# A two-block decoder kernel on one core: how the per-layer embedding projections leave PSUM, and where the sixth tile of the gating products stands

## The reference, cut to what matters

```
g = gelu(y + d_skip * u)
val, gate = split(g @ w_glu, 2)
return val * sigmoid(gate)
```

```
x = x + conv_ffn(h, ffn_w_up[i], ffn_conv_w[i], ffn_conv_b[i], ffn_w_down[i])
gate = sigmoid(rms_norm_2(x, ple_norm[i]) @ ple_w_gate[i])
x = x + gate * (p[i] @ ple_w_proj[i])
```

## Time and profile before

| | |
|---|---|
| median of 3 runs | 2107.18 us (2101.96 to 2107.51) |
| the profiled execution | 2104.71 us, of which span 2102.9 us |
| granted TensorE clock, mean | 0.974 of full speed |
| PE busy | 1988.4 us (95%), 9640 matmuls |
| DVE busy | 1220.0 us (58%) |
| ACT busy | 852.2 us (41%) |
| POOL busy | 442.8 us (21%) |
| chain that ended last | PE 84%, DVE 8%, ACT 5% |

### The profile page before, as it was taken

The page is one execution under the profiler, slowest core; times in us unless marked ns, Lnnn a source line. Parts: engine busy times, 40 slices in busy tenths (PEclk is TensorE's granted clock), DMA queues, the critical chain, the costliest instruction groups (busy, mean ns, idle before and its releaser), DMA issues.

```text
span 2102.9 us, 26554 instructions
## 1 busy us (share of the span) xinstructions
PE 1988.4 (95%) x9640; PEld 1615.3 (77%) x9640; DVE 1220.0 (58%) x1727; ACT 852.2 (41%) x1343; POOL 442.8 (21%) x609
## 2 busy tenths in 40 slices
PE   8999999999999888999999989798777999999988
PEld 8998678888887777877877868686666777878877
DVE  5445465555455994477466456734556666465555
ACT  4323342222235884344244235534665444243333
POOL 3110039998815451100000001100000200000010
PEclk9999899999999999999999999899899999999999
DMA  4221023264442332222323223221111123223232
GB/s 153 84 79 65 21 90 107 85 213 157 167 167 88 121 128 83 87 82 94 105 84 107 81 91 110 92 91 45 51 51 36 61 90 104 87 90 110 80 104 97
DMA packets 65077, 201.64 MB, mean 96 GB/s; under 512 B 6422, under 2 KB 19222, under 8 KB 63948
## 3 DMA queue, kind: packets, MB, share of 16 engines
q1 hardware_dynamic: 57372, 166.39, 23.6%
q0 software_dynamic: 7600, 33.84, 4.5%
HBM read 184.44 MB, written 15.77 MB: 95 GB/s over the span
## 4 chain that ended last, share of the span: by engine, by line
PE 84%; DVE 8%; ACT 5%; issue 2%; DMA 1%; POOL 1%; SPq 0%; ACTq 0%; DVEq 0%; POOLq 0%
PE ps L449 60%; PE ps L587 7%; PE ps L1729 5%; PE ps L738 2%; PE ps L1843 1%; PE ps L438 1%; PE ps L813 1%; DVE w_lo L428 1%; ACT w_hi L424 1%; ACT t L2033 1%; PE ps L1957 1%; DMA cp<-mix_cp 1%; POOL t L529 1%; DMA raw<-in_wstream 1%; PE ps L769 0%
## 5 line engine op out<-in xcount | busy, mean ns | idle before, releaser
L428 DVE TENSOR_TENSOR w_lo<-raw,w_hi 128x1024 fp32r<-128x1024 f32 x308 | 396.7, 1291 | 169.0 <-ACT w_hi L424 168.5
L449 PE MATMUL ps<-x_hi,w_hi 128*128 128x512 f32 x1152 | 458.8, 398 | 3.9 <-DVE w_lo L428 2.6
L449 PE MATMUL ps<-x_lo,w_hi 128*128 128x512 f32 x1152 | 455.7, 396 | 0.0
L449 PE MATMUL ps<-x_hi,w_lo 128*128 128x512 f32 x1152 | 453.5, 394 | 0.0
L424 ACT ACTIVATE w_hi<-raw 128x1024 fp32r<-128x1024 f32 x308 | 322.1, 1049 | 247.5 <-DMA raw<-in_wstream 154.2
L449 PE MATMUL ps<-a_hi,w_hi 128*128 128x512 f32 x704 | 279.8, 397 | 7.7 <-DVE pp L1584 4.8
L449 PE MATMUL ps<-a_hi,w_lo 128*128 128x512 f32 x704 | 279.8, 397 | 0.0
L449 PE MATMUL ps<-a_lo,w_hi 128*128 128x512 f32 x704 | 279.6, 397 | 0.0
L529 POOL TENSOR_TENSOR t<-t,sq 128x512 f32<-128x512 f32 x49 | 72.6, 1483 | 938.4 <-ACT sq L520 936.4
L449 PEld LDWEIGHTS ps<-x_hi,w_hi 128*128 128x128 f32 x1152 | 216.4, 188 | 69.0 <-issue 11.4
L449 PEld LDWEIGHTS ps<-x_hi,w_lo 128*128 128x128 f32 x1152 | 216.7, 188 | 49.8
(11 more groups left out here) (402 smaller groups left out, 3043.0 us busy)
## 6 DMA issues: line engine op xcount, KB each, us to landing
raw<-in_wstream SPq DMA_DIRECT2D x308, 512.0 KB, 3.3
ev<-mix_ev POOLq DMA_DIRECT2D x8, 1024.0 KB, 5.0
mix_cp<-c_p POOLq DMA_DIRECT2D x8, 640.0 KB, 3.4
cp<-mix_cp POOLq DMA_DIRECT2D x8, 640.0 KB, 6.3
mix_ev<-v_b POOLq DMA_DIRECT2D x8, 512.0 KB, 3.5
fall<-fall POOLq DMA_DIRECT2D x4, 544.0 KB, 4.9
h<-in_xT SPq DMA_DIRECT2D x4, 528.0 KB, 6.2
mix_ev<-e_r POOLq DMA_DIRECT2D x1, 2048.0 KB, 9.4
```

The costliest lines, as they stand in the source:

```text
L428: e.tensor_tensor(w_lo[:, u.slot, :], raw[:, u.c % 2, :], w_hi[:, u.slot, :], ALU.subtract)\
L449: last = e.matmul(ps[:, bank, :], wt[:, u.slot, w], x[:, k0 + k, 0:SEQ], start=(k == 0 and n == 0), stop=(k == kt - 1 and n == 2))
```

## The change

The side projection now uses all eight banks. Unit u0 writes banks 4 to 7, unit u0+1 writes banks 0 to 3 in the order in which the next units will need them: `side_bank` gives (u0 + 2 + q) % 4, that is 2, 3, 0, 1 in layer 0 and 0, 1, 2, 3 in layer 1. Each bank's group of 6 matmuls signals when it is done (`pp_mm` for the first three of a unit, `unit_mm` for the fourth), and DVE copies each bank by itself (four copies of 512 columns instead of one of 2048; `pp_ev` counts the first three of a unit, `unit_ev` the fourth). The first side unit no longer waits for `unit_ev`, the second waits for `unit_ev >= u0`, and behind the two PE waits until six of the eight copies are done instead of all. In the gating stage `glu_open_pe` takes a range of tiles: banks 0 and 1 are opened with tiles 0 to 4 ahead of the last tile's output products, and tile 5 follows behind them.

```diff
-    def glu_open_pe(e, s):
+    def glu_open_pe(e, s, k0, k1):
         u = Unit(U_GLU + s)
-        e.wait_ge(lo_ok, u.n(1))
-        e.wait_ge(unit_ev, U_GLU)
-        if s >= 2:
-            e.wait_ge(v_ev, KT)
-        for k in range(GLU_K):
+        if k0 == 0:
+            e.wait_ge(lo_ok, u.n(1))
+            e.wait_ge(unit_ev, U_GLU)
+            if s >= 2:
+                e.wait_ge(v_ev, KT)
+        for k in range(k0, k1):
             if s == 0:
                 e.wait_ge(g_lo, k + 1)
             product(e, u, s, a_hi, a_lo, k, KT)
...
                 u = Unit(u0 + s)
-                e.wait_ge(unit_mm, u.n(1))
-                e.tensor_copy(pp[:, 4 * s:4 * s + 4, :], ps[:, 0:4, :]).then_inc(unit_ev, 1)
+                for q in range(4):
+                    if q < 3:
+                        e.wait_ge(pp_mm, 6 * layer + 3 * s + q + 1)
+                    else:
+                        e.wait_ge(unit_mm, u.n(1))
+                    e.tensor_copy(pp[:, 4 * s + q, :], ps[:, side_bank(u0, s, q), :])                        .then_inc(pp_ev if q < 3 else unit_ev, 1)
                 split_ahead(e, u, split_lo)
         else:
             e.wait_ge(plo_ok, layer + 1)
             for s in range(2):
                 u = Unit(u0 + s)
                 e.wait_ge(lo_ok, u.n(1))
-                e.wait_ge(unit_ev, u.n())
+                if s:
+                    e.wait_ge(unit_ev, u0)
                 for q in range(4):
-                    last = products(e, u, q, p_hi, p_lo, kt=2, w0=2 * q)
-                last.then_inc(unit_mm, 1)
-            e.wait_ge(unit_ev, u0 + 2)
+                    products(e, u, side_bank(u0, s, q), p_hi, p_lo, kt=2, w0=2 * q)                        .then_inc(pp_mm if q < 3 else unit_mm, 1)
+            e.wait_ge(pp_ev, 6 * layer + 6)
+
+    def side_bank(u0, s, q):
+
+        return 4 + q if s == 0 else (u0 + 2 + q) % 4
...
             if i == KT + 1:
-                glu_open_pe(e, 0)
-                glu_open_pe(e, 1)
+                for s in (0, 1):
+                    glu_open_pe(e, s, 0, GLU_K - 1)
             if i >= 2:
                 mixer_back_pe(e, i - 2)
             if i < KT:
                 mixer_tables_pe(e, i)
+        for s in (0, 1):
+            glu_open_pe(e, s, GLU_K - 1, GLU_K)
         for s in (2, 3):
-            glu_open_pe(e, s)
+            glu_open_pe(e, s, 0, GLU_K)
```

More of the change, by code:

```diff
@@ L342, in build @@
     oy_ok = sem("oy_ok")
+    pp_mm = sem("pp_mm")
+    pp_ev = sem("pp_ev")
     wo_mm = sem("wo_mm")
```

## The result

The changed kernel takes 2081.61 us (median of 4 runs, 2080.17 to 2084.19) against 2104.57 us before (4 runs): ratio 0.9886, 95% interval 0.9869 to 0.9903. The forecast was 2085, range 2078 to 2092. Timed again later (e9) it gave 2087.65 (6 runs, 2079.66 to 2091.95), ratio 0.9913 (0.9894 to 0.9932). Of all executions here one, of e3, was slow (5019.69 us at full clock), and it is left out of e3's median. The profiled execution took 2080.17 us, span 2078.4, against 2104.71 and 2102.9 before.

The account below looks back on a forecast made before the run. PE's matmuls bound the kernel (busy 95% of the span), so gains come only from its idle or low-clock time. 9.3 (layer 0) + 7.8 (layer 1) + 4.1 (gating) = 21.2 us; forecast 2085 us, range 2078 to 2092.

Parts of the forecast that it names:

- The first wait of the projection: Side projection: PE's wait for the previous unit's last bank goes, because unit u0 writes banks 4 to 7.
- The second wait: Side projection: PE's wait for unit u0's copy goes; unit u0+1's split weights come with 0.2 us of slack.
- The third wait: Ahead of the first down unit: PE's wait for unit u0+1's copy shrinks to 0.35 us, upper bound 1.6.
- The rule of the Trainium skill: Projection copies: fixed cost per instruction makes four copies 2.76 us and PE's wait near 1 us; forecast used 0.60 each.
- The low clock: Behind the projection's last wait: the clock no longer falls to 0.72, saving 1.7 us in each layer.
- a clock that oscillates with the banks: Rival for the projections and gating: clock stays low when PE cycles banks with micro-idles; 2087 to 2094 us, chance 0.14.
- Nothing is given back behind the projection: Down units: weights come with 3 us of cover, so the projection's gain stays; costed at nothing.
- the 5 that was to be a sign of being wrong: Projection: weight loads over 5 us there would count against the forecast; the longest before was 4.5 us.
- The rival with the weight stream: Down units: weight loads become the bound and the kernel gets slower, 2116 us at loads of 7.2 us; chance 0.03.
- Gating stage, 4.1 us: Gated product: PE waits 2.4 us instead of 6.5, the clock falls, and the closing starts 4.1 us earlier.
- The upper bound of 5.7: Gating stage: the closing starts 5.7 us earlier if the clock stays full.
- The sum: Both projections and gating stage: 21.2 us off, giving 2083.5 from the profiled execution or 2086.0 from the median.

Follow-up runs that it names:

- e9: The changed kernel itself, unaltered, timed again beside two other kernels on one chip: 2087.65 us, ratio 0.9913 to the kernel before.
- e3: The kernel before with the two side units on eight banks but still one copy of 2048 columns per unit: 2095.06 us, ratio 0.9953.
- e4: The kernel before with side projections copied and waited for bank by bank, both units in banks 0 to 3, gating unchanged: 2093.11 us, ratio 0.9949.
- e11: The changed kernel with both side units in banks 0 to 3 again, copied and waited for bank by bank: 2089.85 us, ratio 0.9934.
- e6: The kernel before with 8 unneeded matmuls behind each side unit, filling the waits for the copies: 2102.06 us, ratio 0.9989.
- e2: The kernel before with only the gating part of the change, the new order of the openings: 2100.28 us, ratio 0.9978.
- e7: The changed kernel with the next unit's weights split ahead of the sigmoid on ACT, and likewise earlier on DVE: 2079.15 us, ratio 0.9878.
- e8: The changed kernel with next unit's weights split ahead of the sigmoid, and third and fourth openings' weights one round earlier on ACT: 2080.15 us, ratio 0.9891.
- e10: The changed kernel with next unit's weights split ahead of the sigmoid, timed again beside the changed kernel on one chip: 2077.92 us, ratio 0.9871.
- e5: The changed kernel with tile 5 ahead of the output products again, but behind tiles 0 to 4 of both banks: 2080.52 us, ratio 0.9892.
- e1: The changed kernel with only its projection part, both openings of six tiles again ahead of the output products: 2087.76 us, ratio 0.9920.

## Why the prediction was right, step by step

- *The first wait of the projection goes, 1.1 us a layer.* Right: 1220.02 to 1220.26 without idle time. It is also all that the four more banks give in the traces: e4 and e11 have 25.2 us instead of 24.3 in both layers.
- *The second wait goes, with 0.2 us of slack for the split weights.* Right, the second unit starts 24 steps behind the first. e4 and e11 show that the copies bank by bank would have done it in four banks too: a bank is read long before PE comes back to it.
- *The third wait shrinks to 0.35 us.* It shrank to 0.2: the down unit starts 11.61 us after the last matmul ahead of the projection, and one step and 48 matmuls are 11.39. The distance of 0.60 us that I took from another operation's row holds for the copy to the hundredth. The rule of the Trainium skill (VectorE: DVE Perf Modes, section on the TRN2 errata; 691 ns for each, which the page gives for an fp32 operation on two tensors) agrees with one copy's duration, 0.68, but paid end to end it would be 2.76 us for four, and the trace has 2.48. e3 keeps one copy per unit, and there this wait is 2.38 us, as before.
- *The low clock goes, 1.7 us behind the last wait in each layer.* Right for this pair of executions: 33.6 and 32.1 to 24.3 and 24.2 is 9.3 and 7.8, as forecast. e6 shows that the clock hangs on the waits. e3 shows that it isn't a fixed price of a wait: after one wait alone it didn't fall. The 100 us at full clock that the prediction set against a clock that oscillates with the banks contain no idle time, so they don't test short waits between banks; the 0.94 us ahead of the projections in e4 and e11 do a little, and no fall followed.
- *Nothing is given back behind the projection.* Right: 30 us at clock 1.00 without a gap, longest load 4.1 us, and "to L1" and "to end" carry no trace of it. In e9 one load took 5.2 us, over the 5 that was to be a sign of being wrong, and the columns are the same. The rival with the weight stream is out.
- *Gating stage, 4.1 us.* 5.0 in the trace and 4.6 (2.5 to 6.5) alone. The step that failed is the clock: I took it to fall during the wait of 2.4 us and priced the output products at 4.3 us, from mixer tile 0. They took 2.7 us, in the changed kernel and in e2, e7, e8, e10 and e11. Mixer tile 0 was the wrong row to take it from: there the clock fell at the wait of 2.7 us in all 13 profiled executions, ahead of the last output products, with 2.1 to 2.3 us, in none of five. What makes the two places differ is not shown. The upper bound of 5.7 was the better value; 0.6 of it went into a wait for the weights of the third bank, which I had not seen: DVE's two splits came 0.7 us later, since ACT's last step of tile 6 waited for POOL's rearrangement. With them the last tile's work on DVE came 4.3 us earlier and not 5.0, and since PE came to the closing sooner than forecast, tile 7 was ready 0.5 us before it was read, where the prediction has 2.0 us.
- *The sum.* 21.2 forecast, 22.1 in the three columns. From the profiled execution the forecast of 21.2 makes 2083.5; it took 2080.17, 0.9 from the parts and 2.4 because the stretches that the change doesn't touch were shorter. That 2085 lies between the two medians, 2081.6 and 2087.7, owes something to luck: it was taken between two starting points, and the noise of those stretches is larger than its distance to either.
- *The range.* 2078 to 2092 holds both medians. I had reasoned it from the parts of the change; what makes the width necessary are the stretches that the change doesn't touch, which move by 7 to 8 us from one execution to the next.

## What to carry to other kernels

Where an engine waits for a copy that empties several banks at once, let it wait for the banks one by one before giving it more banks: copies bank by bank in the same four banks gave 15.3 of the 17.1 us (projection columns of e4), more banks with one copy 12.4 (e3), and with the copies cut the additional banks added 0.9 us a layer. These are figures of single traces; the timings, 10.7 us for e4 and 9.9 for e3, don't tell the two apart. Where a wait stands in the middle of independent work, look first at what is queued behind it that doesn't need it; here the order in which the two held pieces came afterwards mattered little (e5). And when an effect is smaller than the spread of the timings, cut each trace at the same instructions and compare the stretches: the projection columns of the same code agree to 0.1 us where medians of five runs differ by 6.

## What the runs showed of the hardware

- Copies of 512 fp32 columns from PSUM take 0.68 us each, but queued behind each other they start every 0.60; one of 2048 takes 2.29. Cut into four, the same copy costs 0.2 us more.
- A standstill of TensorE of 2.1 to 2.9 us is followed by a low clock in some executions and not in others. Of the two waits for the copies in a projection it fell behind the second in all four cases (kernel before and e2, two layers each) and behind the first, as long, in one of four; behind the single wait of e3 in neither layer; behind the closing's wait of 2.9 us in seven of the ten executions that have it, not in e1, e2 and e3; at mixer tile 0, after 2.7 us, in all 13; ahead of the last output products, after 2.1 to 2.3 us, in none of five; in e5, after 2.86 us, not. What decides it stays open; as a term of a sum, 1.6 us is its price and not its expectation. Stretches with the fall, at mixer tile 0 and behind the closing of the changed kernel, and without it, behind the closing of e2 (columns as in the earlier trace rows):

```profile
692.00:698.00 6.00, 4.35 (x25) 4.09 (x25) 5.82 (x9) 3.56 (x9) 4.41 (x8) 0.72 0.67 238
812.00:818.00 6.00, 5.75 (x18) 4.58 (x19) 5.03 (x7) 2.55 (x4) 1.28 (x1) 0.72 0.57 175
```
```profile
810.00:816.00 6.00, 5.13 (x22) 4.21 (x23) 5.02 (x7) 3.18 (x5) 1.29 (x1) 1.00 0.55 175
```

- The stretches "opening" (779.7 to 788.1 us) and "to L1" (737.0 to 743.9) vary from one execution to the next with the same instructions. Of the 5.2 us by which "opening" is longer in the second execution of the changed kernel, 2.1 come in the first 40 us and 2.7 between 234 and 255 us, in the attention of the first block. In "to L1" the granted clock goes with it: from 1500 to 1600 us it is 0.91 in the short execution of the changed kernel and 0.84 in the long one.

```profile
1500.00:1600.00 100.00, 79.66 (x458) 0.91 0.13 40
```
```profile
1500.00:1600.00 100.00, 80.25 (x426) 0.84 0.14 40
```
